# Reordering the waits of a two-layer streaming encoder's feed-forward stages

## The reference

```python
def trunk(x, ...):
    for i in range(DEPTH):
        y = even_mixer(x, ...) if i % 2 == 0 else odd_mixer(x, ...)
        x = layer_norm(ALPHA * x + y, ln_mix_g[i], ln_mix_b[i])
        y, ffb = conv_ffn(x, ff_buf[i], w_ff_in[i], ffconv_w[i], w_ff_out[i])
        x = layer_norm(ALPHA * x + y, ln_ff_g[i], ln_ff_b[i])

def conv_ffn(x, buf, w_in, conv_w, w_out):
    h = x @ w_in                        # 1024 -> 2 x 2816
    gate, up = h[..., :D_FF], h[..., D_FF:]
    gate, buf_new = causal_dwconv(gate, conv_w, buf)   # 3 taps
    return (jax.nn.silu(gate) * up) @ w_out, buf_new

def odd_mixer(x, ...):
    h = x @ w_in                        # 1024 -> 4112, first step of the mixer
    ...
```

## Time and profile before

| | |
|---|---|
| median of 3 runs | 3008.56 us (3004.63 to 3009.67) |
| profiled execution | 3007.08 us |
| its span | 3005.3 us |
| TensorE busy | 96% |
| VectorE, GpSimd, ScalarE busy | 61%, 49%, 28% |
| mean granted TensorE clock | 0.986 |

### The profile page before, as it was taken

The page is one execution under the profiler, slowest core; times in us unless marked ns, Lnnn a source line. Parts: engine busy times, 40 slices in busy tenths (PEclk is TensorE's granted clock), DMA queues, the critical chain, the costliest instruction groups (busy, mean ns, idle before and its releaser), DMA issues. The chain is left out here.

```text
span 3005.3 us, 55758 instructions
## 1 busy us (share of the span) xinstructions
PE 2897.3 (96%) x23320; PEld 2770.5 (92%) x23320; DVE 1826.5 (61%) x3041; ACT 843.5 (28%) x1560; POOL 1479.1 (49%) x1026
## 2 busy tenths in 40 slices
PE   8999999999999999999999979999999999999998
PEld 7999767899999999998999968887889999999998
DVE  2337665585555566678775636666477555556666
ACT  2212475133233320113222223443133333321011
POOL 2233101247777743226732317887546777763224
PEclk9999999999999999999999989999999999999999
DMA  6120102022222242213322234332403222224222
GB/s 180 44 59 16 50 1 89 8 81 65 79 75 77 77 150 104 99 45 102 104 93 88 75 95 107 92 89 54 134 15 105 72 82 67 87 70 172 88 80 75
DMA packets 278416, 243.82 MB, mean 81 GB/s; under 512 B 51305, under 2 KB 251351, under 8 KB 277655
## 3 DMA queue, kind: packets, MB, share of 16 engines
q1 hardware_dynamic: 278167, 240.26, 26.0%
HBM read 177.32 MB, written 62.91 MB: 80 GB/s over the span
## 5 line engine op out<-in xcount | busy, mean ns | idle before, releaser
L160 PE MATMUL ps<-xhi,whi 128*128 128x364 f32 x2352 | 781.5, 332 | 5.7 <-PEq L922 3.6
L161 PE MATMUL ps<-xlo,whi 128*128 128x364 f32 x2352 | 774.9, 329 | 0.0
L166 PE MATMUL ps<-xhi,wlo 128*128 128x364 f32 x2352 | 773.7, 329 | 0.0
L160 PEld LDWEIGHTS ps<-xhi,whi 128*128 128x128 f32 x2352 | 441.8, 188 | 10.7 <-issue 5.9
L161 PEld LDWEIGHTS ps<-xlo,whi 128*128 128x128 f32 x2352 | 442.2, 188 | 3.2 <-issue 0.3
L166 PEld LDWEIGHTS ps<-xhi,wlo 128*128 128x128 f32 x2352 | 441.8, 188 | 1.4
L1591 POOL TENSOR_SCALAR whi<-wraw 128x1024 fp32r<-128x1024 f32 x88 | 111.4, 1266 | 587.5 <-PE ps L166 528.5
L1866 PE MATMUL ps<-xlo,whi 128*128 128x272 f32 (+1 forms) x1216 | 352.1, 290 | 0.0
L1865 PE MATMUL ps<-xhi,whi 128*128 128x272 f32 (+1 forms) x1216 | 351.3, 289 | 0.0
L1867 PE MATMUL ps<-xhi,wlo 128*128 128x272 f32 (+1 forms) x1216 | 351.0, 289 | 0.0
L2378 DVE TENSOR_TENSOR z<-ps,z 128x364 f32<-128x364 f32 x384 | 203.0, 535 | 144.6 <-PE ps L166 144.6
(11 more groups left out here) (513 smaller groups left out, 6670.3 us busy)
## 6 DMA issues: line engine op xcount, KB each, us to landing
wraw<-in_w_ff_in SPq DMA_DIRECT2D x88, 512.0 KB, 4.8
wraw<-in_w_ff_out SPq DMA_DIRECT2D x44, 512.0 KB, 4.0
qkvz<-eo_ob SPq DMA_DIRECT2D x32, 546.0 KB, 4.6
wraw<-in_w_in_o SPq DMA_DIRECT2D x32, 512.0 KB, 4.5
xlo<-hidden SPq DMA_DIRECT2D x28, 546.0 KB, 4.6
hidden<-eo_ups SPq DMA_DIRECT2D x18, 546.0 KB, 2.7
hidden<-oo_ups SPq DMA_DIRECT2D x18, 546.0 KB, 2.8
z<-residual SPq DMA_DIRECT2D x6, 1456.0 KB, 9.5
```

Source lines behind the costliest of these rows:

```text
L160: one = pe.matmul(out, whi, xhi, start=start, stop=False)
L161: two = pe.matmul(out, whi, xlo, start=False, stop=False)
L166: return pe.matmul(out, wlo, xhi, start=False, stop=stop)
```

## The change

It has six parts, all in `layer_block`:

- `square_sums(q - 1)` stands after row 1 of block q on VectorE instead of row 2.
- S2 is the first product of a pair and A11 the second; banks, operand order and waits are renumbered.
- At the start of the output stage SyncE issues the loads of hidden tiles 0 and 1 ahead of the store of tile FT - 2; `reload` moves behind weight unit 2 and waits for hidden tile 1; then comes the store.
- VectorE's first sums go in threes between the taps, silu and gating.
- At the odd mixer, five odd tiles (HEAD = 5) instead of four are multiplied in the interleaved head, product (1, 0) stands ahead of `mean(5)` and (2, 0) ahead of `variance(4)`, ScalarE copies (0, 0), (1, 0) and (2, 0) out ahead of `root(4)`.
- GpSimd splits odd tile 4 ahead of `residual(3)`, (4) and (5), which follow in one piece.

```diff
+    HEAD = 5
-    A11, S2, S3, S1, A12, S4, A22 = range(OPS)
-    BANK = (0, 1, 3, 2, 0, 2, 3)
+    S2, A11, S3, S1, A12, S4, A22 = range(OPS)
+    BANK = (1, 0, 3, 2, 0, 2, 3)
...
+        def kept_place(i, q):
+            return 4 * q + i if i < 4 else 4 * SPL + SPL * (i - 4) + q
         def odd_place(i, q):
-            return 4 * q + i if i < 4 else 4 * SPL + SPL * (i - 4) + q
+            return HEAD * q + i if i < HEAD else HEAD * SPL + SPL * (i - HEAD) + q
...
                 if kind == "out":
-                    if t < 2:
-                        store_hidden(FT - 3 + t)
+                    if t == 0:
+                        store_hidden(FT - 3)
                     if t % CT == 1:
                         for u in range(t - CT + 1, t + 1):
                             load_hidden(u)
-                    if t == 1:
+                    if t == 2:
+                        sp.wait_ge(s("h_in1"), 16)
                         reload()
+                    if t == 2:
+                        store_hidden(FT - 2)
...
-                if (kind, t) == ("odd", 3):
+                if (kind, t) == ("odd", 4):
                     pool.memset(raw[:, :, 0:GAP], 0.0).then_inc(s("raw0"), 1)
-                    residual(3)
-                    residual(4)
-                if (kind, t) == ("odd", 4):
-                    residual(5)
+                    for r in range(SPL, 2 * SPL):
+                        residual(r)
...
-                    pe.wait_ge(s("odd_free"), odd_place(i - 2, q) + 1)
+                    pe.wait_ge(s("odd_free"), kept_place(i - 2, q) + 1)
...
                 odd_product(0, 0)
+                odd_product(1, 0)
                 mean(5)
-                odd_product(1, 0)
+                odd_product(2, 0)
                 variance(4)
-                odd_product(2, 0)
                 odd_product(3, 0)
+                odd_product(4, 0)
                 odd_product(0, 1)
                 odd_product(1, 1)
                 variance(5)
-                odd_product(2, 1)
-                odd_product(3, 1)
-                for i in range(4):
+                for i in range(2, HEAD):
+                    odd_product(i, 1)
+                for i in range(HEAD):
                     odd_product(i, 2)
...
-                kept(0, 0)
+                for i in range(3):
+                    kept(i, 0)
                 root(4)
-                kept(1, 0)
                 for k in range(KD):
                     high(4, k)
                     if k % 2:
                         squares(5, k // 2)
-                kept(2, 0)
                 kept(3, 0)
...
-                    if q >= 1 and j == 2:
+                    if q >= 1 and j == 1:
                         square_sums(q - 1)
...
-            sums(0)
-            sums(1)
+            for seq in range(0, 3):
+                sums(seq)
             tap(t, 1)
-            sums(2)
+            for seq in range(3, 6):
+                sums(seq)
             tap(t, 2)
-            sums(3)
-            sums(4)
+            for seq in range(6, 9):
+                sums(seq)
             silu(t)
-            sums(5)
+            for seq in range(9, 12):
+                sums(seq)
             gated_up(NPR - 1)
```

More of the change, by code:

```diff
@@ L1708, in _ @@
                     elif kind == "out" and t < 4:
-                        pool.wait_ge(s("prod"), products(NPR - 1, 1, (S2, S1, S4, A22)[t]))
+                        pool.wait_ge(s("prod"), products(NPR - 1, 1, (A11, S1, S4, A22)[t]))
                     elif kind == "out":
@@ L1802, in _ @@
             MOVING = [
-                ((m.xhi, m.xlo), 0, 0), ((t2hi, t2lo), 0, None), ((t3hi, t3lo), 0, None), ((t1hi, t1lo), 0, None),
+                ((t2hi, t2lo), 0, None), ((m.xhi, m.xlo), 0, 0), ((t3hi, t3lo), 0, None), ((t1hi, t1lo), 0, None),
                 ((m.xhi, m.xlo), HQ, 0), ((m.xhi, m.xlo), HQ, 1), ((t4hi, t4lo), 0, None)]
@@ L1854, in block_product @@
                 if i == 0 and e == 0 and j in (S1, S2, S3):
-                    pe.wait_ge(s("t_lo"), {S2: 1, S3: 2, S1: 3}[j])
+                    pe.wait_ge(s("t_lo"), {S1: 1, S2: 2, S3: 3}[j])
                 if i == 0 and e == 0 and j == A22:
@@ L2006, in _ @@
                 variance(5)
-                odd_product(2, 1)
-                odd_product(3, 1)
-                for i in range(4):
+                for i in range(2, HEAD):
+                    odd_product(i, 1)
+                for i in range(HEAD):
                     odd_product(i, 2)
-                for i in range(4, NODD):
+                for i in range(HEAD, NODD):
                     for q in range(SPL):
@@ L2090, in sigmoid @@
                 if k == 3:
-                    act.wait_ge(s("odd_free"), odd_place(i, SPL - 1) + 1)
+                    act.wait_ge(s("odd_free"), kept_place(i, SPL - 1) + 1)
                 act.activation(sg[:, :], (gb[:, 0:TW] if k == 3 else cv[:, :]), ACT.Sigmoid).then_inc(s("sig_odd"), 1)
@@ L2189, in _ @@
             gates_kept(2)
+            operand_high(0, S2)
             operand_high(0, A11)
-            operand_high(0, S2)
             operand_high(0, S3)
@@ L2206, in _ @@
                 if more:
-                    operand_high(i + 1, A11)
+                    operand_high(i + 1, S2)
                 first_kept(i, 1)
                 if more:
-                    for j in (S2, S3, S1, A12):
+                    for j in (A11, S3, S1, A12):
                         operand_high(i + 1, j)
@@ L2551, in _ @@
             convolve(t)
-            sums(0)
-            sums(1)
+            for seq in range(0, 3):
+                sums(seq)
             tap(t, 1)
-            sums(2)
+            for seq in range(3, 6):
+                sums(seq)
             tap(t, 2)
-            sums(3)
-            sums(4)
+            for seq in range(6, 9):
+                sums(seq)
             silu(t)
-            sums(5)
+            for seq in range(9, 12):
+                sums(seq)
             gated_up(NPR - 1)
-            for seq in range(6, DONE):
+            for seq in range(12, DONE):
                 if seq % CHUNK in (12, 13):
@@ L2643, in conv_odd @@
                 x = raw[:, k, :]
-                dve.wait_ge(s("odd_free"), odd_place(i, SPL - 1) + 1)
+                dve.wait_ge(s("odd_free"), kept_place(i, SPL - 1) + 1)
                 for r in range(3):
```

## The result

| | before | after |
|---|---|---|
| median | 3009.07 us (4 runs) | 2988.96 us (4 runs, 2988.94 to 2991.01) |
| ratio | | 0.9938, interval [0.9921, 0.9955] |
| profiled execution, its span | 3007.08, 3005.3 us | 2988.97, 2987.2 us |
| mean granted clock | 0.986 | 0.990 |

With all later runs of the two kernels the medians are 3008.1 us (73 runs) and 2989.8 us (8 runs), 18.3 us apart.

A forecast was written before the change was run, and what follows sets the result against it. TensorE, busy 96%, was taken as the bound. Terms 12.4 + 0 + 0.6 - 3.7 = 9.3 us won gave 2997.8 us against the profiled time, 2999.3 against the median; 8-in-10 range 2993 to 3006.

The forecast's parts named there:

- Squares at the second row: Mixer output: earlier square sums cut the 5.4 us variance waits to 1.4; 12.4 us won with clock, between 5.0 and 15.3.
- (a): Rival at the squares: the clock falls despite the shorter variance wait, taking back 4.4 us: 3003.7 us; chance 0.17.
- (c): Rival at the squares: sums still caught by a split, three times, and the clock falls: 3006.7 us, no difference; chance 0.07.
- (e): Rival at the squares: the sums meet no split at all and the wait is gone: 2996.4 us; chance 0.05.
- S2 first: FFN pairs: the new product order leaves TensorE without a wait, met with 0.16 us of slack; term 0.
- (d): Rival in the pairs: ScalarE waits for GpSimd's sum, A12 starts late; slower, 1 us each gives 3035; chance 0.07.
- h ahead of a store: Output stage: first group 0.7 us later per layer, layer 0's z waits go; term +0.6 us, between -3 and +3.
- Odd mixer: Mean's 4.31 us wait goes, a 2.5 us wait for a ScalarE copy comes; term -3.7 us, between -6 and +2.
- (b): Rival at the odd mixer: normalising slowed throughout, wait at (4, 1) grows; term -6, outputs' start -1.5: 3003.7 us; chance 0.14.
- The clock: Behind TensorE's waits: no drop after 1.30 us, a drop after 2.43, so none expected after 1.4; 4.4 us counted won.

The follow-up runs named there:

- experiment 1: The kernel before with one edit, square sums after row 1 instead of row 2: 2992.19 us against 3008.58, ratio 0.9944.
- experiment 2: The kernel before with S2 first, the new order on SyncE's queue and the sums in threes: 3003.10 us, ratio 0.9980.
- Experiment 12: The kernel before with S2 first and the new order on SyncE's queue, sums left single: 3005.08 us against 3007.15, ratio 0.9990.
- experiment 10: The kernel after, with GpSimd holding the second FFN split until block 1's square sums are done: 2991.81 us, ratio 0.9947.
- experiment 3: The kernel before with only the odd mixer's part (HEAD = 5, order of odd products and copies, residual in one piece): 3010.01 us, ratio 1.0005.

## Why the prediction was wrong, point by point

By the runs of the single parts, 11.2 us were won beyond the forecast: 4.9 in the output stages, 4.0 in the squares and 2.3 at the odd mixer, the last two within the doubt of those runs.

- **Squares at the second row: right.** 12.4 us forecast, 12.3 and 11.5 in the pairs of profiles, 11.7 in experiment 1's profile. The runs of experiment 1 give 16.4 us with an interval from 12.0; what the 4 us more are is not known. Waits of 1.5 us for 1.4, sums of 7.8 us for 7.75, no fall of the clock behind it. Rivals (a), (c) and (e) did not come.
- **S2 first: nearly right.** 0.4 us lost per layer for 0, no wait in a pair. Rival (d) did not come.
- **h ahead of a store: this step failed.** The term of +0.6 us measured 5.5 (3.0 to 8.7) by the runs of experiment 2, S2's loss included, and 4.3 and 8.4 us in the two pairs of profiles. I took the move of weight unit 2 ahead of the reload for a loss of 0.7 us per layer, by its cast in the way of low half 1. That loss is there (0.45 us). But I followed the moved split only to its new place and not away from its old one beside the taps, where the earlier trace rows shows it, and so put what its leaving changes there at nothing. Experiment 12, S2 and this order without the threes, wins 2.1 us (0.6 to 5.7) where my sum has a loss of 1.4; by which of the two ways named there stays open. The other error was to count one profile's layer 1, where the waits for sums were 0.26 and 0.78 us, as what the kernel pays: it pays about 3 us more. And part of what the profiles show is luck: 1.7 us in layer 0 in both pairs, and as much in layer 1 in the second, are a fall of the clock behind the first group that came before and not after.
- **Odd mixer: right in its mechanism, too dear by 2 us.** The mean's wait went, the wait for (2, 1)'s copy came (2.2 us for 2.5), but the clock stayed up behind it (1.7 us counted). In experiment 10 it did fall. I also put a price at nothing without a reason: I counted the clock behind the new wait, but not behind the old one of 4.31 us. In before it stood at 0.57 for the 4 us behind it, 1.7 us that go with the wait (its row stands below). The last variance came 2.3 us later for 3.5, with a product of 4.0 us more done: 1.7 us won for 0.5. Most of this is that clock, since of the 4.45 us that TensorE waited between mean(4) and the last variance 3.57 are left, in smaller waits. The 3.5 holds a slip: by its 0.3 us a pair, eight pairs are 2.4 us and not 2.8. Behind it 3.2 us were lost, 2.8 of them in two waits (2.17 and 0.60 us). Rival (b) did not come.

```profile
1374.00:1378.00 4.00, 4.00 (x13) 3.46 (x14) 4.00 (x2) 0.00 (x0) 3.81 (x4) 0.57 0.51 131
```

- **The clock.** I read it as a threshold between 1.30 and 2.43 us. Waits of 2.2 to 2.9 us bring it down in some executions and not in others. In experiment 3 it even fell to 0.50 at 1393.3, right behind three waits of 0.27, 0.64 and 0.65 us in 3 us; in the six profiles of after and its variants the same three waits brought no fall. A fall behind one wait of 2.2 to 2.9 us leaves 0.57 to 0.69 over the next 4 us, so the wait has a price of 1.2 to 1.7 us times a chance, and a single profile shows one throw. Together with the order of arrival above it moves the sums of the profiles by up to 4 us against each other. It is the likely reason, not a shown one, why 1.0 to 2.4 us won at one wait could not be found in the time.

Still open is what makes up the rest between the sums of the profiles (18.3 and 16.5 us) and the medians (18.3 us apart over all runs, 20.1 in the first four). It is within what the runs scatter.

## What to carry to other kernels

When an instruction is moved, follow what it leaves as well as what it meets: a GpSimd split that no longer runs beside VectorE's two-input work can be worth several us, and moving it onto another such chain gives most of it back. Put VectorE's short sums in groups that empty several banks ahead of each long instruction, so that TensorE feels less of a stretched one (2.0 us of waits for 3.1 to 4.1 in layer 1 here, a gain in time too small to be clear). Before a forecast rests on one profile, look for places where two engines arrive within a few tenths of a microsecond of each other, and for waits of 2 to 3 us, and give both outcomes a price. Give the clock behind a wait that goes the same price as the clock behind one that comes.

## What the runs showed of the hardware

- Who comes first between VectorE and GpSimd can hang on 0.1 us. With the tap 0.10 us ahead of the cast TensorE waited 1.0 us for sums in the stage, with the cast 0.72 us ahead 3.1 us, and the stage was 3.5 us longer, a fall of the clock included. Even the first tap, which reads one tensor, takes 0.79 us alone and 2.41 us beside a subtraction on GpSimd (experiment 2: 2708.15, before: 2711.35).
- The granted clock after the same wait of 2.88 us at the same instruction was 0.65 in one execution and 1.00 in another. Behind the wait of 2.45 us near the end (line 1978 of before) it was 0.50 to 0.61 over 4 us in all 14 profiles.
- The 25 us behind the longest wait, at the start of the delta rule (17.3 to 17.6 us), had a mean granted clock of 0.65 and 0.71 in two executions of the same kernel, and 0.81 in experiment 1, with the same code.
